# Two blocks of a transformer on one core: first unit by pieces, own operand columns for the last feed-forward trip, no fillers at the first block's seams

## The chip, the cores and the metric

The kernel runs on one core of one Trainium2 chip. The metric is the device time of one execution in microseconds (us); the median of repeated executions is what counts.

## What is computed

256 tokens of width 1024 go through two blocks, all in float32. The reference, cut to its skeleton:

```python
def first_block(x, ...):                    # DEPTH = 2 layers
    for i in range(DEPTH):
        h = h + 0.5 * swiglu(rmsnorm(h), ffn1)           # d_ff 2816
        u = rmsnorm(h)                                   # w_in: conv, low-rank q/kv, two gates
        merged = sigmoid(g_conv) * short_conv(u) + sigmoid(g_mla) * mla_attention(u)
        h = h + merged @ w_o
        h = h + 0.5 * swiglu(rmsnorm(h), ffn2)
        h = h + sigmoid(rmsnorm(h) @ w_ple_gate) * (p @ w_ple_proj)
    return rmsnorm(h)

def second_block(x, ...):                   # a layer with GLA, then one with NSA
    for i in range(DEPTH):
        h = gla_mixer(x) if i == 0 else nsa_mixer(x)
        x = layer_norm(ALPHA * x + h)
        x = layer_norm(ALPHA * x + moe_ffn(x))           # 16 experts in 4 groups, top 2
```

## The kernel before

Everything sits in SBUF as features on 128 partitions by 256 tokens; `h` is the residual stream. The program is five instruction streams written by hand, one per engine, that meet in semaphores; program order on each engine is the order of execution. Weights come as a stream of **units** of 128x2048 floats (1 MB). SP fetches each unit in two halves into one of three `raw` slots. ACT rounds it to `w_hi` (`split_hi`), DVE writes the rest as `w_lo` (`split_lo`), and PE takes the unit (`take`). Activations are split in the same way, into `x_hi`/`x_lo` or `y_hi`/`y_lo`, so one exact product is three matmuls (hi by hi, hi by lo, lo by hi; `product`, L1897). The splits run two units ahead of PE, and the slot of a unit is the one of the unit three before it.

A **dense** unit (`columns`) multiplies two blocks of 128 output columns by 8 pieces of the operand: 48 matmuls of 256 columns. The operand becomes ready in four pieces of two (`PIECES`), one `x_ready` each. With `first_wait=STARTS` PE waits for a piece where the first output block needs it; the second block is done only after the first.

A **feed-forward** stage has 11 trips of 256 hidden columns. A trip of PE is `gate_up(0)` (gate), `gate_up(1)` (up), each 16 pairs of matmuls (L1994 with 512 and L1995 with 256 columns), and `down` of the trip before (48 matmuls). DVE and ACT make the hidden operand in between: DVE `side` (L1239), ACT its rounding (L866), DVE the rest (L1244). That operand has two columns of 256, always the same ones, so ACT waits for the `down` before it. The last `down` stands behind the loop, after six fillers. A **filler** (`keep_warm`, L1946) is a matmul of zeros whose result nobody reads.

`units(n, after)` of DVE is: split of a coming unit, wait for a result, use of the result (`after`). With `early=True` the last of them uses the result first and splits behind it.

The stages that the change touches are called **seams** here, where PE goes from one stage to the next and needs an operand made from the last result: end of ffn1 to `w_in`; the rope of the queries (`query`, L1406 to L1416, which reads PSUM banks that the keys' unit writes next); `w_mla_out` to `w_o` (`merge`, L1429); `w_o` to ffn2 (`residual`, L1438); end of ffn2; the embedding gate to the next layer's ffn1 or, after the second layer, to GLA; and in the second block the start and end of an expert stage (`moe`) and the start of NSA. The layer loop runs the first block's code twice. An expert stage has 20 tiles of three units; POOL copies token slots of a run of four tiles (`copy_runs`, L691) and PE reads three register values (`value_load`) that tell which slots a run uses.

## Time and profile before

| | |
|---|---|
| median of 3 runs (lowest to highest) | 2005.53 us (2005.04 to 2006.02) |
| time of the profiled execution | 2010.71 us |
| its span | 2008.9 us |
| PE, DVE, ACT, POOL busy | 98%, 71%, 55%, 2% of the span |
| granted clock, mean over the span | 0.99 |

PE is the engine to watch: its busy share holds the fillers and whatever runs at half clock, so 98% is not 98% useful. The useful views are who PE waits for, the stretches around each seam instruction by instruction, and the granted clock of short stretches.

### The profile page before, as it was taken

The page shows a single profiled execution, that of the slowest core. Times are in us where ns is not written, and L with a number is a line of the kernel's source. Part 1 is how long each engine was busy: PE and PEld are TensorE (multiplying, and loading weights), DVE is VectorE, ACT ScalarE, POOL GpSimd, SP SyncE. Part 2 cuts the span into 40 slices and gives each one's busy share as a digit, 9 for nine tenths or more (in the row PEclk, how much of TensorE's full clock was granted, in tenths as well). Part 3 has the DMA queues.
Part 4 walks back from the last instruction along what each step waited for, and adds up shares of the span by engine and source line. Part 5 has one row for each costly group of instructions (what it writes and reads, how often), then busy time and mean ns, then how long its engine had stood idle before and what let it go on. Part 6 is the DMA issues. An engine that isn't in the chain of part 4 may idle for free.

```text
span 2008.9 us, 34438 instructions
## 1 busy us (share of the span) xinstructions
PE 1969.5 (98%) x12986; PEld 1775.3 (88%) x12986; DVE 1434.0 (71%) x1812; ACT 1099.2 (55%) x1449; POOL 33.6 (2%) x37
## 2 busy tenths in 40 slices
PE   9999999999999999999999999999999999999999
PEld 7999998989988999999988999888888788997887
DVE  6666876666667766786666667685788877568886
ACT  6444645454447544545545446434677643646775
POOL 0000000000000000000000000000100011001000
PEclk9999999999999999999999999999999999999999
DMA  7655554346554655555345556352799744027993
GB/s 280 200 185 187 178 196 148 130 157 196 184 185 161 192 185 187 191 184 171 115 164 179 188 188 191 123 163 69 277 367 366 288 126 139 9 96 307 367 368 140
DMA packets 89662, 388.03 MB, mean 193 GB/s; under 512 B 10096, under 2 KB 10096, under 8 KB 74832
## 3 DMA queue, kind: packets, MB, share of 16 engines
q1 hardware_dynamic: 88992, 383.87, 55.9%
q0 software_dynamic: 560, 2.67, 0.3%
q8 instruction: 73, 1.20, 0.2%
q14 instruction: 37, 0.30, 0.1%
HBM read 385.45 MB, written 1.05 MB: 192 GB/s over the span
## 4 chain that ended last, share of the span: by engine, by line
PE 89%; DVE 5%; ACT 2%; issue 2%; DMA 1%; DVEq 1%; SPq 0%; ACTq 0%
PE psa L1897 36%; PE psd L1897 19%; PE psa L1994 16%; PE psa L1995 8%; DMA raw<-weights 1%; DVE w_lo L1142 1%; PE psa L2522 1%; PE psa L2195 1%; DVEq L1127 1%; PE psd L1939 1%; PE psd L2531 1%; PE psa L2100 0%; PE psd L2049 0%; DVE x_both L1155 0%; PE psd L2215 0%
## 5 line engine op out<-in xcount | busy, mean ns | idle before, releaser
L1142 DVE TENSOR_TENSOR w_lo<-raw,w_hi 128x1024 fp32r<-128x1024 f32 x500 | 593.4, 1229 | 128.3 <-ACT w_hi L758 125.9
L1897 PE MATMUL psa<-x_both,w_hi 128*128 128x256 f32 x1984 | 366.3, 287 | 9.2 <-DVE x_both L1147 4.2
L758 ACT ACTIVATE w_hi<-raw 128x1024 fp32r<-128x1024 f32 x250 | 262.7, 1051 | 181.4 <-PE psa L1897 179.5
L1897 PEld LDWEIGHTS psa<-x_both,w_hi 128*128 128x128 f32 x1984 | 313.1, 194 | 13.3 <-DVE x_both L1155 5.6
L1897 PE MATMUL psa<-x_both,w_lo 128*128 128x256 f32 x992 | 282.4, 285 | 0.0
L760 ACT ACTIVATE w_hi<-raw 128x1024 fp32r<-128x1024 f32 x250 | 261.3, 1045 | 3.5 <-DMA raw<-weights 3.5
L1994 PE MATMUL psa<-x_both,w_hi 128*128 128x512 f32 x704 | 248.4, 395 | 4.1 <-DVE x_both L1155 1.7
L1994 PE MATMUL psa<-y_both,w_hi 128*128 128x512 f32 x704 | 249.6, 396 | 1.6 <-DVE y_both L1155 1.6
L1897 PE MATMUL psa<-w_hi,slots_x 128*128 128x512 f32 x640 | 204.8, 401 | 0.0
L1995 PE MATMUL psa<-x_both,w_lo 128*128 128x256 f32 x704 | 197.7, 281 | 0.0
L1995 PE MATMUL psa<-y_both,w_lo 128*128 128x256 f32 x704 | 196.8, 280 | 0.0
L1897 PEld LDWEIGHTS psa<-x_both,w_lo 128*128 128x128 f32 x992 | 192.1, 194 | 0.0
L1994 PEld LDWEIGHTS psa<-x_both,w_hi 128*128 128x128 f32 x704 | 132.6, 188 | 34.6 <-issue 3.6
L1994 PEld LDWEIGHTS psa<-y_both,w_hi 128*128 128x128 f32 x704 | 132.1, 188 | 33.2 <-DVE y_both L1155 2.2
L1897 PE MATMUL psd<-y_both,w_hi 128*128 128x256 f32 x816 | 151.2, 286 | 4.7 <-DVE w_lo L1142 4.3
L1137 DVE TENSOR_TENSOR w_lo<-raw,w_hi 128x2048 fp32r<-128x2048 f32 x60 | 137.5, 2292 | 16.2 <-ACT w_hi L753 14.0
L1897 PE MATMUL psd<-x_both,w_hi 128*128 128x256 f32 x768 | 139.1, 283 | 0.4 <-DVE x_both L1244 0.4
L1897 PEld LDWEIGHTS psa<-w_hi,slots_x 128*128 128x128 f32 x640 | 117.2, 188 | 25.0
L1897 PEld LDWEIGHTS psd<-y_both,w_hi 128*128 128x128 f32 x816 | 128.3, 192 | 6.9 <-DVE w_lo L1142 4.7
L1995 PEld LDWEIGHTS psa<-x_both,w_lo 128*128 128x128 f32 x704 | 133.7, 190 | 0.1
L1995 PEld LDWEIGHTS psa<-y_both,w_lo 128*128 128x128 f32 x704 | 132.1, 188 | 0.2
L1897 PE MATMUL psa<-w_lo,slots_x 128*128 128x512 f32 x320 | 126.8, 396 | 0.0
(402 smaller groups left out, 3452.4 us busy)
## 6 DMA issues: line engine op xcount, KB each, us to landing
raw<-weights SPq DMA_DIRECT2D x500, 512.0 KB, 5.0
raw<-weights SPq DMA_DIRECT2D x60, 1024.0 KB, 5.3
raw_y<-weights SPq DMA_DIRECT2D x36, 1024.0 KB, 5.2
x<-weights SPq DMA_DIRECT2D x18, 1024.0 KB, 4.9
h<-x_in SPq DMA_DIRECT2D x1, 1024.0 KB, 5.2
result<-h SPq DMA_DIRECT2D x2, 512.0 KB, 2.9
sml<-smalls POOLq DMA_DIRECT2D x1, 831.0 KB, 10.3
cst<-consts POOLq DMA_DIRECT2D x1, 747.5 KB, 7.7
```

The source lines that it names most:

```text
L758: act.activation(w_hi[:, s, UNIT_HALVES[0]], raw[:, s, UNIT_HALVES[0]], ACT.Copy).then_inc(hi_done, 1)
L760: act.activation(w_hi[:, s, UNIT_HALVES[1]], raw[:, s, UNIT_HALVES[1]], ACT.Copy).then_inc(hi_done, 1)
L1127: dve.drain()
L1137: dve.tensor_tensor(w_lo[:, s, :], raws[r], w_hi[:, s, :], ALU.subtract).then_inc(lo_done, 2)
L1142: dve.tensor_tensor(w_lo[:, s, c], raw[:, s, c], w_hi[:, s, c], ALU.subtract).then_inc(lo_done, 1)
L1897: ins = pe.matmul(out, lhs, rhs, start=first and n == 0, stop=last and n == 2, skip_group_check=True)
L1939: ins = pe.matmul(out, ones, src[:, k, :], start=k == 0, stop=k == n - 1)
L1994: pe.matmul(out, hi, operand[2][:, :, k, :], start=k == 0, stop=False, skip_group_check=True)
L1995: ins = pe.matmul(out[:, 0:T], lo, operand[0][:, k, :], start=False, stop=k == KD - 1, skip_group_check=True)
L2195: ins = pe.matmul(out[:, P * tt:P * tt + keys], a, b, start=False, stop=tt == 1 and n == len(terms) - 1, skip_group_check=True)
L2522: ins = pe.matmul(out[:, P * tt:P * tt + keys], nsa_q[:, i, tt * P:tt * P + P], (nsa_ks, nsa_kw)[branch][:, i // 4, side_of, 0:keys], star ...
L2531: ins = pe.transpose(psd[:, t % 2, P * i:P * i + P], nsa_probs[:, t % 3, P * i:P * i + P], ident)
```

## The change

It joins these edits. (1) `columns` with `STARTS` and the first `gate_up` of a feed-forward stage take the operand piece by piece: all output blocks of a piece before the next piece. (2) The last trip of a feed-forward stage is written out behind the loop (9 trips in the loop and one behind it where there were 10), and its hidden operand goes to columns 2 and 3 of the buffer, so it need not wait for the `down` before it; the split of the next stage's unit comes behind it on ACT and DVE. (3) The 6, 8 and 8 fillers at the seams of the first block go; in an expert stage's start 5 and 9 become 8 and 6. (4) `query` makes its four products first and writes them to `x32`; the combining comes after the next split. (5) `merge` and `residual` lose `early=True`. (6) In the first expert stage's last tile two of the three splits of coming units move behind the tile's hidden operand, one of them behind the layer norm. (7) The NSA gates' 16 products are made during the layer norm, piece by piece, in another PSUM bank, with a semaphore `mix_known` of their own. (8) POOL's copy for run r waits for the r+1st `turn` of the stage, and PE's register reads come one per tile. The diff of these, cut to its core:

```diff
                 for run in range(1, EG):
+                    pool.wait_ge(moe_turned, layer * TILES + run + 1)
...
-                def trip(first):
+                def trip(first, last=False):
...
+                    if last:
+                        act.wait_ge(side_ready, seen.more(side_ready))
+                        act.activation(hid_to[:, 2:4, :], side[:], ACT.Copy).then_inc(hid_hi, 1)
+                        split_hi()
+                        seen.more(unit_done, tag="result")
+                        return
...
-                with seen.loop(act, label, trips - 1):
+                with seen.loop(act, label, trips - 2):
                     trip(False)
+                trip(False, last=True)
...
                     silu(n)
-                    if more or not last:
+                    if more:
                         split_hi()
...
                     hidden_hi(n)
-                    if more:
+                    if more or not last:
                         split_hi()
...
             token_norm(1, scattered, turn_rest, split=True)
-
+            split_hi()
...
-                    if not first:
+                    if not first and not last:
                         split_lo()
                         seen.more(unit_done, tag="result")
+                    to = slice(2, 4) if last else slice(0, 2)
                     dve.wait_ge(hid_hi, seen.more(hid_hi))
-                    dve.tensor_tensor(hid[1][:, 0:2, :], side[:], hid[0][:, 0:2, :],
+                    dve.tensor_tensor(hid[1][:, to, :], side[:], hid[0][:, to, :],
                                       ALU.subtract).then_inc(hid_ready, 1)
+                    if last:
+                        split_lo()
+                        seen.more(unit_done, tag="result")
...
+                turned_q = q_rot.rearrange("p (i e) t -> p i e t", e=2)
+                r1_cos, r2_sin, r2_cos, r1_sin = (x32[:, 2 * i:2 * i + 2, :] for i in range(4))
+
                 def query(j):
-                    c = cos1.unsqueeze(1).broadcast_to([P, 2, T])
-                    s = sin1.unsqueeze(1).broadcast_to([P, 2, T])
                     r1, r2 = four(0, psd)[:, 0:2, :], four(0, psd)[:, 2:4, :]
-                    dve.tensor_tensor(rope_a[:], r1, c, ALU.mult)
-                    step(dve.tensor_tensor(rope_b[:], r2, s, ALU.mult))
-                    turned_q = q_rot.rearrange("p (i e) t -> p i e t", e=2)
-
-                    def combine(to, combined):
-                        for e, part in enumerate((first, second)):
-                            ins = dve.tensor_tensor(turned_q[to, :, e, :], rope_a[part], rope_b[part], combined)
-                        return ins
-                    step(combine(first, ALU.subtract))
-                    dve.tensor_tensor(rope_a[:], r2, c, ALU.mult)
-                    step(dve.tensor_tensor(rope_b[:], r1, s, ALU.mult))
-                    return combine(second, ALU.add)
+                    for dst, r, table in ((r1_cos, r1, cos1), (r2_sin, r2, sin1), (r2_cos, r2, cos1),
+                                          (r1_sin, r1, sin1)):
+                        ins = dve.tensor_tensor(dst, r, table.unsqueeze(1).broadcast_to([P, 2, T]), ALU.mult)
+                    return ins
                 units(1, query)
-                units(3, None)
+                units(1, None)
+                settle()
+                for to, a, b, combined in ((first, r1_cos, r2_sin, ALU.subtract), (second, r2_cos, r1_sin, ALU.add)):
+                    for e, part in enumerate((first, second)):
+                        dve.tensor_tensor(turned_q[to, :, e, :], a[part], b[part], combined)
+                units(2, None)
...
-                units(4, merge, early=True)
+                units(4, merge)
...
-                units(4, residual, early=True)
+                units(4, residual)
...
+            def by_pieces(s, outs, x, ready):
+
+                for piece in PIECES:
+                    pe.wait_ge(ready, seen.more(ready))
+                    for j, out in enumerate(outs):
+                        for k in range(*piece):
+                            c = (k * len(outs) + j) * P
+                            ins = product(out, parts(s, c, c + P), (x[0][:, k, :], x[1][:, k, :]),
+                                          j == 0 and k == 0, k == KD - 1)
+                ins.then_inc(unit_done, 1)
...
+                if first_wait == STARTS:
+                    by_pieces(s, outs, x, ready)
+                    return
...
+                    def block(j, ks):
                         out = psa[:, 2 * bank + j, :]
-                        for k in range(KD):
-                            if j == 0 and k in waits:
-                                pe.wait_ge(x_ready, seen.more(x_ready))
+                        for k in ks:
                             hi, lo = parts(s, (2 * k + j) * P, (2 * k + j + 1) * P)
                             pe.matmul(out, hi, operand[2][:, :, k, :], start=k == 0, stop=False, skip_group_check=True)
                             ins = pe.matmul(out[:, 0:T], lo, operand[0][:, k, :], start=False, stop=k == KD - 1,
                                             skip_group_check=True)
-                        if bank == 1 and j == 0:
+                        return ins
+
+                    s = take()
+                    if waits:
+                        for piece in PIECES:
+                            pe.wait_ge(x_ready, seen.more(x_ready))
+                            for j in range(2):
+                                ins = block(j, range(*piece))
+                    else:
+                        ins = block(0, range(KD))
+                        if bank == 1:
                             ins.then_inc(first_half, 1)
+                        ins = block(1, range(KD))
...
-                            ins = product(out, parts(s, c, c + P), (hid[0][:, k, :], hid[1][:, k, :]),
+                            at = k + 2 if last else k
+                            ins = product(out, parts(s, c, c + P), (hid[0][:, at, :], hid[1][:, at, :]),
...
-                with seen.loop(pe, label, trips - 1):
-
+                def trip():
                     pe.wait_ge(gate_scaled, seen.more(gate_scaled))
                     gate_up(0)
                     pe.wait_ge(side_ready, seen.more(side_ready))
                     gate_up(1)
                     down(False)
+
+                with seen.loop(pe, label, trips - 2):
+                    trip()
+                trip()
                 seen.more(side_ready)
-                pe.wait_ge(gate_scaled, seen.more(gate_scaled))
-                keep_warm(6, psa_of(0))
+                seen.more(gate_scaled)
                 down(True)
...
-                keep_warm(5, psd_of(3))
+                keep_warm(8, psd_of(3))
...
-                keep_warm(9, psd_of(3))
+                keep_warm(6, psd_of(3))
...
-                        pe.wait_ge(group_known, seen.more(group_known))
-                        second = [pe.value_load(second_block[0:1, run:run + 1], min_val=0, max_val=1)
-                                  for run in range(EG - 1)]
                     turn(n - 1)
                     gate_up(n, 1)
+                    if n == 1:
+
+                        pe.wait_ge(group_known, seen.more(group_known))
+                    if n < EG:
+                        second.append(pe.value_load(second_block[0:1, n - 1:n], min_val=0, max_val=1))
                     down(n - 1)
...
-                keep_warm(8, psd_of(0))
                 dense(4, KD, 2, x, signal=None, first_wait=STARTS)
-                keep_warm(8, psd_of(0))
                 feed_forward("ffn2", FF_TRIPS, y, x)
...
-            seen.more(even_normed, 2)
+
+            w_gates = small("w_gates").rearrange("p (k c) -> p k c", k=KD)
+            for j, piece in enumerate(PIECES):
+                ready = (even_normed, odd_normed)[j % 2]
+                pe.wait_ge(ready, seen.more(ready))
+                for k in range(*piece):
+                    for tt in range(TT):
+                        ins = pe.matmul(psd[:, 0, tt * 48:(tt + 1) * 48], h[:, k, tt * P:tt * P + P], w_gates[:, k, :],
+                                        start=k == 0 and tt == 0, stop=k == KD - 1, skip_group_check=True)
+            ins.then_inc(pe_to_act, 1)
...
-            w_gates = small("w_gates").rearrange("p (k c) -> p k c", k=KD)
-            for tt in range(TT):
-                for k in range(KD):
-                    ins = pe.matmul(psa[:, 2, tt * 48:(tt + 1) * 48], h[:, k, tt * P:tt * P + P], w_gates[:, k, :],
-                                    start=k == 0, stop=k == KD - 1, skip_group_check=True)
-            ins.then_inc(pe_to_act, 1)
```

DVE in the rope of the queries, before (`side` and `act_gate` are scratch, `psd` holds the queries' unit, `arena` the tables or the turned queries):

```order
L1142 TENSOR_TENSOR w_lo<-raw,w_hi 128x1024 [waits hi_done]
L1212 REGISTER_ALU
L1406 TENSOR_TENSOR side<-psd,arena 128x512 [waits unit_done]
L1407 TENSOR_TENSOR act_gate<-psd,arena 128x512
L1119 REGISTER_ALU
L1412 TENSOR_TENSOR arena<-side,act_gate 64x2x256 [waits dve_step]
L1412 TENSOR_TENSOR arena<-side,act_gate 64x2x256
L1119 REGISTER_ALU
L1415 TENSOR_TENSOR side<-psd,arena 128x512 [waits dve_step]
L1416 TENSOR_TENSOR act_gate<-psd,arena 128x512
```

The same place now, where `x` is the scratch `x32`:

```order
L1151 TENSOR_TENSOR w_lo<-raw,w_hi 128x1024 [waits hi_done]
L1221 REGISTER_ALU
L1423 TENSOR_TENSOR x<-psd,arena 128x512 [waits unit_done]
L1423 TENSOR_TENSOR x<-psd,arena 128x512 x3
L1150 REGISTER_ALU
L1151 TENSOR_TENSOR w_lo<-raw,w_hi 128x1024 [waits hi_done]
L1150 REGISTER_ALU
L1151 TENSOR_TENSOR w_lo<-raw,w_hi 128x1024 [waits hi_done]
L1430 TENSOR_TENSOR arena<-x 64x2x256 x4
```

The split of the keys' unit moved ahead of the four combining instructions. DVE at the last `merge`, before:

```order
L1429 TENSOR_TENSOR side<-psa,arena 128x512 [waits unit_done]
L1119 REGISTER_ALU
L1430 TENSOR_TENSOR x<-x,side 128x512 [waits dve_step]
L1146 REGISTER_ALU
L1147 TENSOR_TENSOR x_both<-x,x_both 128x512 [waits xh_ready]
L1141 REGISTER_ALU
L1142 TENSOR_TENSOR w_lo<-raw,w_hi 128x1024 [waits hi_done]
L1141 REGISTER_ALU
L1142 TENSOR_TENSOR w_lo<-raw,w_hi 128x1024 [waits hi_done]
```

And now:

```order
L1151 TENSOR_TENSOR w_lo<-raw,w_hi 128x1024 [waits hi_done]
L1221 REGISTER_ALU
L1441 TENSOR_TENSOR side<-psa,arena 128x512 [waits unit_done]
L1128 REGISTER_ALU
L1442 TENSOR_TENSOR x<-x,side 128x512 [waits dve_step]
L1155 REGISTER_ALU
L1156 TENSOR_TENSOR x_both<-x,x_both 128x512 [waits xh_ready]
L1155 REGISTER_ALU
L1156 TENSOR_TENSOR x_both<-x,x_both 128x512 [waits xh_ready]
```

The split that stood between the last two pieces of the operand (`x_both`) stands before the last result now. ACT in the last tile of the first expert stage, before (`act_gate` is the tile's silu, `x_both<-psa` its hidden operand):

```order
L890 ACTIVATE act_gate<-psa 128x256 [waits unit_done]
L758 ACTIVATE w_hi<-raw 128x1024 [waits unit_done,raw_full1]
L760 ACTIVATE w_hi<-raw 128x1024 [waits raw_rest1]
L758 ACTIVATE w_hi<-raw 128x1024 [waits unit_done,raw_full2]
L760 ACTIVATE w_hi<-raw 128x1024 [waits raw_rest2]
L894 ACTIVATE x_both<-psa 128x256 [waits moe_turned]
```

And now:

```order
L899 ACTIVATE act_gate<-psa 128x256 [waits unit_done]
L903 ACTIVATE x_both<-psa 128x256 [waits moe_turned]
L760 ACTIVATE w_hi<-raw 128x1024 [waits unit_done,raw_full1]
L762 ACTIVATE w_hi<-raw 128x1024 [waits raw_rest1]
L912 ACTIVATE slots_x<-psd 128x512 [waits moe_out]
```

The hidden operand comes before both splits now, and the second of them is no longer here.

## Rows read from the trace of the kernel before

**Rows 1.** The page: busy time and share of each engine.

```profile
PE 1969.5 (98%) x12986; PEld 1775.3 (88%) x12986; DVE 1434.0 (71%) x1812; ACT 1099.2 (55%) x1449; POOL 33.6 (2%) x37
```

**Rows 2.** Waits of PE: waiting line, releaser, us in total, times, longest.

```profile
PE psd L1897 <- DVE w_lo L1142: 4.3, 2, 2.1
PE psa L1897 <- DVE x_both L1147: 4.2, 4, 1.8
PE psa L1897 <- DVE x_both L1155: 4.2, 4, 2.2
...
PE psd L1897 <- DVE x_both L1633: 2.9, 1, 2.9
...
PE psa L2144 <- DVE arena L1680: 0.9, 1, 0.9
```

**Rows 3.** Stretches: us, each engine's busy us (instructions), PEclk, DMA share, GB/s.

```profile
321.90:325.30 3.40, 3.40 (x18) 3.40 (x17) 3.40 (x4) 0.00 (x0) 0.00 (x0) 0.50 0.96 261
325.30:328.40 3.10, 3.10 (x27) 3.10 (x26) 0.08 (x1) 0.00 (x0) 0.00 (x0) 1.00 0.92 296
...
1271.41:1277.62 6.21, 6.21 (x29) 6.21 (x30) 5.07 (x6) 5.07 (x5) 0.00 (x0) 0.50 0.02 3
...
1601.90:1605.30 3.40, 3.40 (x10) 2.62 (x10) 0.69 (x1) 0.65 (x2) 0.00 (x0) 0.50 0.95 389
```

**Rows 4.** Chain of waits, the downs of two trips in a row: start, us, what.

```profile
38.63 5.75 PE psd L1897 x48
55.49 5.76 PE psd L1897 x48
```

**Rows 5.** Timeline of PE, end of ffn1: start, us, what, [idle before].

```profile
195.97 1.47 PE L1946 MATMUL psa<-zero 128*128 128x512 bf16 x6
...
210.47 0.81 PE L1939 MATMUL psd<-x,cst 128*128 128x256 f32 x3
```

**Rows 6.** Timeline of DVE at the same end of ffn1.

```profile
192.22 0.69 DVE L1239 TENSOR_TENSOR side<-side,act_gate 128x512 f32<-128x512 f32 x1
...
200.32 1.29 DVE L1260 SCALAR_TENSOR_TENSOR h<-psd,h 128x512 f32<-128x512 f32 x2 [0.19 <-issue]
...
208.90 0.69 DVE L1163 TENSOR_TENSOR x<-x 128x512 f32<-128x512 f32 x1
```

**Rows 7.** Timeline of DVE in the rope of the queries.

```profile
312.99 0.69 DVE L1406 TENSOR_TENSOR side<-psd,arena 128x512 f32<-128x512 f32 x1 [0.18 <-issue]
...
318.48 3.50 DVE L1142 TENSOR_TENSOR w_lo<-raw,w_hi 128x1024 fp32r<-128x1024 f32 x3
```

**Rows 8.** Timeline of PE, then DVE, from w_mla_out to w_o.

```profile
388.37 1.90 PE L1946 MATMUL psd<-zero 128*128 128x512 bf16 x8
...
390.50 2.35 DVE L1142 TENSOR_TENSOR w_lo<-raw,w_hi 128x1024 fp32r<-128x1024 f32 x2
392.77 0.68 DVE L1147 TENSOR_TENSOR x_both<-x,x_both 128x512 fp32r<-128x512 f32 x1
```

**Rows 9.** Timeline of PE, then DVE, from w_o to ffn2.

```profile
414.49 1.90 PE L1946 MATMUL psd<-zero 128*128 128x512 bf16 x8
...
416.09 2.35 DVE L1142 TENSOR_TENSOR w_lo<-raw,w_hi 128x1024 fp32r<-128x1024 f32 x2
```

**Rows 10.** Timeline of DVE, then PE, from the embedding to the next ffn1.

```profile
645.93 0.69 DVE L1163 TENSOR_TENSOR x<-x 128x512 f32<-128x512 f32 x1
...
649.27 0.59 PE L1939 MATMUL psd<-x,cst 128*128 128x256 f32 x2
```

**Rows 11.** Timeline of ACT in the last tile of the first expert stage.

```profile
1596.70 1.06 ACT L758 ACTIVATE w_hi<-raw 128x1024 fp32r<-128x1024 f32 x1 [1.48 <-DMA raw<-weights]
...
1598.97 0.37 ACT L894 ACTIVATE x_both<-psa 128x256 fp32r<-128x256 f32 x1
```

**Rows 12.** One line: the gates' products (ns min/median/max, first and last start, shape).

```profile
L2431 PE MATMUL psa<-sml,h x32: 208/275/275, 1654.3 to 1657.7; 128*128 128x48 f32 x32
```

**Rows 13.** Timeline of DVE beside POOL's first copy of an expert stage.

```profile
1427.51 1.79 DVE L1680 TENSOR_TENSOR arena<-arena 128x32 f32<-128x32 f32 x1
```

33 lines of the change are left out of this document (18 added, 15 removed).

## The prediction

> **What bounds the kernel now.** The page comes first: PE is busy 98% of the span and DVE 71% [rows 1]. So time can leave only through PE: its waits, its fillers, and the stretches where its clock is low. The waits of PE come next [rows 2]. They are few and each sits at a seam: four waits for an operand piece in a dense first unit with 4.2 us in all for each of two lines, two of 2.1 for a weight split, one of 2.9 for the hidden operand of the last expert tile. Then the stretches [rows 3]: after a wide wait the granted clock stands at 0.50 (1.2 GHz) where it is 1.00 (2.4 GHz) otherwise. In 3.40 us at 0.50 PE starts 18 products, in 3.10 us at 1.00 it starts 27, so the low stretch is worth about 3.40 - 18 x 3.10/27 = 1.3 us lost; with the records at its ends left out (16) it is 1.5. I take **1.4 us for one low stretch** and twice that for the 6.2 us one. Last, the timelines around each seam [rows 5 to 13].
>
> Unit prices: 48 products of 256 columns take 5.76 us, 0.12 each, and a trip takes 55.49 - 38.63 = 16.86 us [rows 4], so a gate or up unit is (16.86 - 5.76)/2 = 5.55, or 0.35 for each of its 16 pairs. A piece of one block is 6 x 0.12 = 0.72 in a dense unit and 2 x 0.35 = 0.7 in a gate unit.
>
> **The sum, seam by seam, in us of the profiled execution.** (a) *End of ffn1, twice.* Six fillers and a 0.21 wait stand between the last two `down` [rows 5]: the next product could start at 195.97 and starts 1.68 later. DVE's `side` is done at 192.91 [rows 6]. With columns of its own ACT can round at once (0.63) and DVE subtract (0.7), so the operand is there at about 194.4, before 195.97, and the whole 1.68 goes from this place. What is late next is DVE: the first residual starts at 200.32 because the split of the unit after next lies before it, and that split waits for the slot that the first of the two `down` frees at 196.1. It moves up by the 0.6 by which ACT no longer rounds first, to 199.7. The sum of squares is ready at 208.90 + 0.69 = 209.6 now and 9.3 after that residual; the product over it starts at 210.47. In future it starts at about 209.0, since PE, with both blocks of each piece done as it comes, is through at 208.1. The gain is 210.47 - 209.05 = 1.4; the ends are 0.6 (only DVE's shift) and 2.4 (PE alone). Twice: **2.8**.
>
> (b) *Rope, twice.* DVE holds the queries from 312.99 to 318.48, and PE's keys' unit waits 2.1 for the split behind them [rows 7, 2]. Four products of 0.69 now end at 315.7, and the split (2.36 for two halves) at 318.1, before PE gets there at 318.76. The combining (2.8) comes next, then the split for the values' unit, done at 323.4, which PE needs a keys' unit (5.76) after 318.76, at 324.5. So it has 1.1 left. With the wait of 2.1 goes the low stretch behind it [rows 3]: 2.13 + 1.4 = 3.5. Twice: **7.0**. The lower end, with the clock still low, is 2 x 2.1.
>
> (c) *w_mla_out to w_o, twice.* Eight fillers start at 388.37; the eight hold PE 1.55 before the unit begins at 389.92. Then it waits until 393.5 for the last piece, which DVE makes at 392.77 because the late split (390.50, 2.35) is ahead of it [rows 8]. The split goes into the idle time before the result (it is ready at 384.8), so the last piece is ready at 391.4. PE starts at 388.4 and spends 1.44 on each piece: 389.8, 391.3, then the third piece (ready 390.6), the fourth at 392.7, end 394.2. Now it ends at 389.92 + 5.76 + 1.4 of waits = 397.1. Gain 2.9, twice, with the start 0.1 earlier: **6.0**. (d) *w_o to ffn2, twice.* The same pattern: fillers from 414.49 cost 1.55, and the split at 416.09 stands before the last piece [rows 9]; a wait of 0.8 and the 0.5 of restarts follow. PE now goes through 16 pairs from 414.5 and ends at 420.1 where it ended at 422.9: 2.8, **5.6**. The cover of both is the same: the split must end before the unit's result, with 1.2 to spare in (c).
>
> (e) *End of ffn2, twice.* 1.68 goes as in (a), but the first weight split that the embedding gate needs comes behind DVE's operand and moves only by the same 0.6: **1.2**. (f) *Embedding to ffn1, once.* Half of each of the first two pieces, 2 x 0.7, moves into waits, and a low stretch (1.4) would go. The sum of squares is ready at 646.62 and PE takes it at 649.27 [rows 10]; the gain cannot pass 2.6, and four clears (0.65) come first: **2.3**, or 1.3 with a low stretch. (g) *Embedding to GLA, once.* 2 x 0.72 into waits, and one of the two low stretches of 1271.41 to 1277.62 [rows 3]: **2.8**, ends 2.0 and 3.2.
>
> (h) *Start of the expert stages.* POOL's copy blocks a small product of DVE, 1.79 in place of the 0.19 of its neighbours [rows 13]. In the second stage PE waits 0.9 for that line [rows 2]; in the first it costs 0.5 of a split. Both go; fillers moved from the second place to the first cost about 0.25 each: **0.9**. A register read on PE is hidden behind the products queued before it. (i) *End of the first expert stage.* The hidden operand is rounded at 1598.97, after splits that wait for DMA [rows 11]. The tile's `turn` is done at 1595.9, so the operand is ready at 1596.8 and PE, busy with the first scatter until 1597.8, does not wait: 2.9 [rows 2] and the low stretch behind it [rows 3], 1.4 to 1.5: **4.4**. (j) *Start of NSA.* The gates' 32 passes took 3.6 [rows 12]. They now lie ahead of NSA's first unit; of them 0.9 fits into the longest wait of 1.8 [rows 2], the other 2.7 delay it, and 3.6 goes later, where PE waits 1.6 for a split already. So what comes back is bounded by DVE: between -2 and +2. I take **0**.
>
> **A rule that speaks against part (8).** The row first: beside POOL's copy a DVE product with both inputs in SBUF lasted 1.79 [rows 13]. The copies now run within the tile loop, where nearly every DVE instruction is such a split. The Trainium skill (SBUF — State Buffer, section SBUF: two separate sides) says that VectorE and GpSimd share one port pair under an exclusive lock, that a VectorE operation with two SBUF inputs takes part in it against a GpSimd operation that reads SBUF, and that the later one is fully blocked. By that rule, with which the row agrees, six copies of 1.9 would block up to 11 us of DVE. Not all of it would reach PE: my estimate, from DVE's idle share, is at most 0.9 a copy, 5.4 in all, and a time of 1978. The sum goes by 0, since before the change the second and third copies lay on DVE's work too and PE showed no wait for a split there; 5.4 stays in the range.
>
> **Sum.** 2.8 + 7.0 + 6.0 + 5.6 + 1.2 + 2.3 + 2.8 + 0.9 + 4.4 + 0 = 33.0. The profiled execution took 2010.71, 5.2 above the median of 2005.53 as profiled ones do here; less 33.0 it is 1977.7, and the median **1972.5 us** (faster by 1.6%).
>
> **Rivals.** *1. The clock takes part of it back.* Each filler-free seam may have its own low stretch. For: a wait of 2.1 was enough for one [rows 2, 3], and 0.9 to 1.4 us of waiting is left in (a), (f) and (g), with small products of low activity in (j). Against: in (b), (c) and (d) nothing is left to wait for. Six to nine stretches at 1.4 give 1981 to 1985. *2. The splits do not get there in time.* If the late split in (c) and (d) and the one in (b) still end after PE arrives, by a DMA or a slot, only the fillers and half of the waits go: 3.3 + 3.1 + 3.1 + 4.2 for the first block, about 20 with the rest, 1985 to 1988. For: margins of 1.1 and 1.2. Against: these margins are read from finish times in one timeline. *3. Better:* NSA gives its 2 and (a), (g) reach their upper ends: 1966. *4. Slower than before:* the fillers are what holds the clock in the first block. Its ten seams without fillers would each fall to 1.2 GHz and stay through two stretches and more, as after 1270.8. At 1.4 for a stretch the gain of 33 is gone at 24 stretches; with 28 the time is 2011. Against it: PE has real work in their place. *5. It does nothing:* the waits come from what I did not see, such as fetching instructions for the longer layer body.
>
> **How the numbers follow.** Forecast 0.74 (band 1968 to 1979); rival 1 0.12; rival 2 0.05; rival 3 0.05; rival 4 0.02; rival 5 0.02. The range 1965 to 1984 takes in the forecast's band with the 5.4 of the copies, rival 3 and most of rival 1. About 0.2% (4 us) is what a measurement of this kernel can tell from no change: faster 0.96, same 0.02, slower 0.02.
>
> **What would show it.** In the profile after: no wait of PE at the keys' unit and no low stretch behind it; w_o and ffn2 starting at the spacing of products after the unit before; the two last `down` as 96 products in a row; the last expert `down` directly behind the first scatter; a wait of about 1 us for the folded squares after ffn1; POOL's copies beside longer DVE splits without a wait of PE. It is wrong if the fillers' places show gaps, if low stretches number more than eight, or if NSA's first unit starts over 3 us later against the layer norm.

## Result: 1976.4 us, and the profile after

| | before | changed kernel |
|---|---|---|
| median (lowest to highest) | 2005.28 us (2003.93 to 2006.02), 4 runs | 1976.36 us (1974.0 to 1978.56), 4 runs |
| ratio | 1 | 0.9855, 95% interval 0.9841 to 0.9868 |
| profiled execution | 2010.71 us | 1976.19 us |
| stretches of PE at 1.2 GHz in it | 37.5 us | 13.7 us |

The forecast was 1972.5 with a range of 1965 to 1984. The kernel is faster, by 28.9 us of median where 33.0 were forecast, and the two profiled executions lie 34.5 apart. That these two differences disagree by 5.6 us is the first thing to explain, and the experiments begin there.

The page of the changed kernel, PE's row and the others, to hold beside [rows 1]:

```profile
PE 1944.7 (98%) x12919; PEld 1760.6 (89%) x12930; DVE 1433.3 (73%) x1812; ACT 1099.1 (56%) x1449; POOL 36.7 (2%) x37
```

DVE and ACT do what they did; PE's busy time is 24.8 us shorter. So most of the gain (24.8 of 34.5) is not waiting that went but busy time that went: fillers, and work at 1.2 GHz. The waits of PE by releaser, to hold beside [rows 2]:

```profile
PE psa L1910 <- DVE w_lo L1151: 5.8, 4, 2.0
PE psa L1910 <- DVE x_both L1164: 3.0, 4, 1.5
PE psd L1966 <- DVE x L1172: 1.6, 3, 0.7
...
PE psa L2018 <- DVE w_lo L1151: 1.5, 1, 1.5
```

The line of 4.3 for the split behind the queries and the one of 2.9 for the last expert operand are gone. New are the waits for the folded squares (1.6), which the prediction had named as what is late next after ffn1, two of 1.1 for a split after ffn2, inside the 5.8, and one of 1.5 for a split where the second layer starts. Next come two stretches of the changed kernel at the times of the first and the last of [rows 3] (other instructions run there by now), and the three in which its clock is low (us, each engine's busy us, PEclk, DMA share, GB/s):

```profile
321.90:325.30 3.40, 3.40 (x21) 2.94 (x20) 1.91 (x2) 2.21 (x2) 0.00 (x0) 1.00 0.83 258
...
1383.70:1387.12 3.42, 3.42 (x17) 3.31 (x17) 3.18 (x11) 1.99 (x4) 0.00 (x0) 0.50 1.02 429
1585.10:1591.92 6.82, 6.74 (x31) 6.74 (x32) 5.32 (x5) 4.45 (x6) 4.18 (x6) 0.50 0.38 123
1601.90:1605.30 3.40, 3.40 (x31) 3.40 (x30) 3.23 (x5) 3.17 (x5) 0.00 (x0) 1.00 0.56 188
1772.82:1776.24 3.42, 3.20 (x13) 2.26 (x13) 2.96 (x14) 2.97 (x5) 0.00 (x0) 0.50 1.00 417
```

The first block, which lost its fillers, has no low stretch in this execution. The three that are left (13.7 us) lie around the layer norms and routers of the second block.

The end of ffn1, to hold beside [rows 5, 6], DVE first and then PE:

```profile
197.03 2.36 DVE L1151 TENSOR_TENSOR w_lo<-raw,w_hi 128x1024 fp32r<-128x1024 f32 x2 [0.34 <-ACT w_hi L760]
199.58 1.29 DVE L1274 SCALAR_TENSOR_TENSOR h<-psd,h 128x512 f32<-128x512 f32 x2 [0.19 <-issue]
...
208.16 0.69 DVE L1172 TENSOR_TENSOR x<-x 128x512 f32<-128x512 f32 x1
```

```profile
208.90 1.13 PE L1966 MATMUL psd<-x,cst 128*128 128x256 f32 x4 [0.70 <-DVE x L1172]
```

The residual starts at 199.58, behind the split (199.7 was forecast); PE takes the squares at 208.90 (209.05 was forecast) after a wait of 0.70. The rope, beside [rows 7]:

```profile
311.52 2.48 DVE L1423 TENSOR_TENSOR x<-psd,arena 128x512 f32<-128x512 f32 x4 [0.18 <-issue]
313.93 2.35 DVE L1151 TENSOR_TENSOR w_lo<-raw,w_hi 128x1024 fp32r<-128x1024 f32 x2
316.37 2.79 DVE L1430 TENSOR_TENSOR arena<-x 64x512 f32<-64x512 f32 x4
```

Four products, the split, the combining. The split ends at 316.3, and PE begins the keys' unit at 317.1 without waiting. At w_o, beside [rows 8], the last two operand pieces lie side by side and the split is elsewhere:

```profile
384.58 1.47 DVE L1156 TENSOR_TENSOR x_both<-x,x_both 128x512 fp32r<-128x512 f32 x2
386.31 2.36 DVE L1151 TENSOR_TENSOR w_lo<-raw,w_hi 128x1024 fp32r<-128x1024 f32 x2 [0.26 <-ACT w_hi L760]
```

**The account by seam.** The same instruction of PE was looked up in the trace of before and of the changed kernel at the end of each seam, and the difference of its start times was taken from one seam to the next. The first pair is the two profiled executions above, the second is one more execution of each (the first two experiments).

| step of the sum | forecast | first pair | second pair |
|---|---|---|---|
| (a) end of ffn1, twice | 2.8 | 2.7 | 2.7 |
| (b) rope, twice | 7.0 | 7.6 | 6.1 |
| (c), (d) w_o and ffn2, twice | 11.6 | 11.7 | 11.7 |
| (e) end of ffn2, twice | 1.2 | 1.1 | 1.1 |
| (f) embedding to ffn1 | 2.3 | 1.6 | 0.5 |
| (g) embedding to GLA | 2.8 | 3.2 | 2.0 |
| (h) starts of the expert stages | 0.9 | 1.7 | 0.3 |
| (i) end of the first expert stage | 4.4 | 4.6 | 4.1 |
| (j) start of NSA | 0 | 0.2 | 0.2 |
| the first microseconds, GLA | - | 0.1 | -1.2 |
| sum | 33.0 | 34.5 | 27.4 |

With another instruction taken as the end of a seam these figures move by up to 0.2. Where only instructions and fillers moved (a, c, d, e), both pairs agree with each other and with the sum within 0.2 us. Where a low stretch went (b, f, g, i, which the sum had with one or two each, and h, where it had none), the pairs differ by up to 1.5.

### The profile page after: what moved, and what is told of

The parts are those of the page before. It is cut to its first block, busy times and chain, and to the rows that moved or that the text cites. A ratio compares the mean times of both kernels' runs of the same rounds, so it can differ in the third digit from the quotient of the medians.

```text
span 1974.4 us, 34273 instructions
## 1 busy us (share of the span) xinstructions
PE 1944.7 (98%) x12919; PEld 1760.6 (89%) x12930; DVE 1433.3 (73%) x1812; ACT 1099.1 (56%) x1449; POOL 36.7 (2%) x37
## 4 chain that ended last, share of the span: by engine, by line
PE 90%; DVE 5%; ACT 2%; issue 1%; DVEq 1%; DMA 0%; ACTq 0%; SPq 0%
PE psa L1910 37%; PE psd L1910 19%; PE psa L2018 16%; PE psa L2019 8%; DVE w_lo L1151 1%; PE psa L2564 1%; PE psa L2236 1%; DVEq L1136 1%; PE psd L1966 1%; ACT w_hi L760 1%; PE psd L2573 1%; PE psa L2138 0%; PE psd L2119 0%; PE psd L2256 0%; PE psd L2087 0%
```

## Experiments

Each kernel was timed beside the kernel before. Times are medians with the lowest and the highest run, ratios are against before. The changed kernel had 1974.0 to 1978.6 in eight runs.

**Before, profiled again.** No edit.

> The kernel before, unchanged, profiled a second time. Question: the first profiled execution took 2010.71, 5.2 above the median of 2005.5, and the sum was made against it. Theory A (that execution had more stretches at 1.2 GHz than most): it had nine stretches with 37.5 us in all, mean granted clock 0.990; at 1.4 us lost for 3.4, an execution of 2005.5 has some 12.6 us less of it, 25 us, mean clock 0.994, and the profiled one here lies wherever its number of stretches puts it. Theory B (the profile itself costs some 5 us on this kernel): profiled again about 2010 with the unprofiled runs at 2005. Median 2005 +- 1.5 by both.

Measured: 2005.78 (2003.92 to 2007.06, 11 runs), with 15 more of before between 2002.34 and 2007.35. The profiled execution took 2005.07, with a mean granted clock of 0.993 against 0.990 and eight stretches, 27.3 us where the first had nine with 37.5. So theory A holds: the first profiled execution, 2010.71, was above all 26 others, and the second profiled one, 2005.07, lies in the middle of them, so a profile as such doesn't cost 5 us. The rope's wait in both layers and the stretch behind each show how that comes about (us, busy us of PE, its loads, DVE, ACT and POOL, PEclk, DMA share, GB/s):

```profile
318.20:320.33 2.13, 0.00 (x1) 0.00 (x1) 2.13 (x3) 2.10 (x3) 0.00 (x0) 1.00 0.05 12
320.33:323.73 3.40, 3.40 (x28) 3.40 (x29) 3.40 (x4) 0.82 (x1) 0.00 (x0) 1.00 0.90 290
944.12:946.26 2.14, 0.00 (x1) 0.00 (x1) 2.14 (x3) 2.10 (x3) 0.00 (x0) 1.00 0.06 8
947.40:950.80 3.40, 3.40 (x18) 3.40 (x17) 3.35 (x3) 0.00 (x0) 0.00 (x0) 0.50 0.77 245
```

The wait is the same, 2.13 and 2.14. Behind the first PE runs on at 2.4 GHz and starts 28 products, behind the second it runs at 1.2 GHz and starts 18. In the first profile [rows 3] it was low behind the first as well. So a wait of 2.1 lowers the clock in some executions and not in others, and a low stretch behind it is a price with a chance, not a fixed one.

**The changed kernel again.** No edit.

> The changed kernel, unchanged, as the yardstick for the others here. Median 1976 +- 2, ratio 0.9855. Its first profiled execution (1976.2) had three stretches of 1.2 GHz with 13.7 us in all, none in the first block. Theory A says that the number moves between executions: 3 to 6 stretches of 3.4. A rival (the clock's falls sit at fixed places of the program): the same three places, near 1384, 1585 and 1773.

Measured: 1976.17 (1974.73 to 1977.67), ratio 0.9851 (0.9836 to 0.9866). Four stretches, 17.1 us: the same three places 1.6 us later and one more, behind a wait of GLA that both kernels have. Of the changed kernel's first profile and of this one:

```profile
1287.07:1289.04 1.97, 0.00 (x0) 0.00 (x0) 1.92 (x2) 1.97 (x3) 0.00 (x0) 1.00 0.07 10
1289.04:1292.44 3.40, 3.40 (x15) 2.79 (x16) 3.13 (x3) 2.29 (x3) 0.00 (x0) 1.00 0.80 265
```

```profile
1287.53:1289.50 1.97, 0.00 (x1) 0.00 (x0) 1.92 (x2) 1.97 (x3) 0.00 (x0) 1.00 0.07 10
1289.71:1293.12 3.41, 3.41 (x9) 2.63 (x9) 3.25 (x3) 2.09 (x3) 0.00 (x0) 0.50 0.84 269
```

The same program, the same wait of 1.97, and PE starts 15 products behind it at full clock once, 9 at half clock the other time. Both expectations hold in part: the stretches near 1384, 1586 and 1773 are in both profiles, this one is not.

**The rope alone**, in the kernel before.

```diff
+                    for dst, r, table in ((r1_cos, r1, cos1), (r2_sin, r2, sin1), (r2_cos, r2, cos1),
+                                          (r1_sin, r1, sin1)):
+                        ins = dve.tensor_tensor(dst, r, table.unsqueeze(1).broadcast_to([P, 2, T]), ALU.mult)
...
                 units(1, query)
-                units(3, None)
+                units(1, None)
+                settle()
+                for to, a, b, combined in ((first, r1_cos, r2_sin, ALU.subtract), (second, r2_cos, r1_sin, ALU.add)):
+                    for e, part in enumerate((first, second)):
+                        dve.tensor_tensor(turned_q[to, :, e, :], a[part], b[part], combined)
+                units(2, None)
```

> The kernel before with edit (4) alone: four products of the query first, the combining after the next split. Theory: the wait of 2.1 at the keys' unit goes in both layers (4.2) and the stretch of 1.2 GHz behind it (2 x 1.4), 7.0 in all: 1998.5. Rival: the clock's fall is not caused by that wait and turns up elsewhere: 4.2 only, 2001.3, with as many low stretches as before. Rival 2: the split comes late all the same: 2005.

Measured: 2000.79 (1994.89 to 2001.42, 5 runs), ratio 0.9966 (0.9952 to 0.9979): 4.8 us by the medians, 6.8 by the ratio with an interval from 4.2 to 9.6. That takes in both the 7.0 of the theory and the 4.2 of the first rival, so the time doesn't decide between them. The place itself does: in the second layer, where before's second profile has the low stretch, the instruction behind the rope starts 3.9 earlier against that profile, in the first, where it has none, 2.4. The stretches behind the keys' unit's start:

```profile
318.20:322.00 3.80, 3.80 (x34) 3.80 (x33) 3.76 (x5) 2.92 (x3) 0.00 (x0) 1.00 0.69 235
947.00:951.00 4.00, 4.00 (x30) 3.73 (x30) 3.51 (x4) 1.21 (x1) 0.00 (x0) 1.00 0.60 186
```

PE is busy all the time and at full clock. The waits (4.2) went, and with them what low stretches stood behind them. But the whole profile has as many stretches as before's second, eight, with 34.1 us where that has 27.3, one of them 6.8 us long behind a wait of 1.65 at 637, where before's second profile has none. So the rival's last clause came true in this execution. Its five runs spread over 6.5 us, with mean clocks of 0.991 to 0.997 in them: what is left of the kernel before has its own low stretches, some in one execution and some in another.

**Fillers put back** in the changed kernel, 6, 8 and 8.

```diff
-                seen.more(gate_scaled)
+                pe.wait_ge(gate_scaled, seen.more(gate_scaled))
+                keep_warm(6, psa_of(0))
                 down(True)
...
+                keep_warm(8, psd_of(0))
                 dense(4, KD, 2, x, signal=None, first_wait=STARTS)
+                keep_warm(8, psd_of(0))
                 feed_forward("ffn2", FF_TRIPS, y, x)
```

> The changed kernel with the 6, 8 and 8 fillers of the first block put back at their places. Theory: eight fillers cost 1.55 each time (four times, 6.2), since nothing waits there any more; of the 1.68 before the last `down` 1.2 lies in the waits of 0.5 and 0.7 that the changed kernel has behind it after ffn1, and 1.1 in the one after ffn2, so 0.5 and 0.6 each, 2.2 in all. Sum 8.4: 1984.8. Rival (the fillers hold the clock up, which takes part of the gain back without them): the first block of the changed kernel has low stretches in other executions that the fillers remove; then less than 8.4, down to 0 at six stretches. Rival 2: the waits behind are set by DVE's chain that moves with PE, so the fillers cost their whole 1.68: 12.9, 1989.

Measured: 1983.24 (1982.73 to 1983.34), ratio 0.9888 (0.9873 to 0.9903): 7.1 slower than without. The eights are all of it: against the second profile of the changed kernel PE becomes 3.4 later at w_o and ffn2 of the first layer and 3.4 in the second, 6.9 in all, 1.72 for each eight where 1.55 was reckoned (the 1.55 until the next product starts, and that product takes 0.31 in place of 0.12 to the next). The sixes, for which 2.2 was expected, cost nothing that shows, after ffn1 or after ffn2. After ffn1:

```profile
195.62 1.47 PE L1973 MATMUL psa<-zero 128*128 128x512 bf16 x6
...
208.78 1.13 PE L1966 MATMUL psd<-x,cst 128*128 128x256 f32 x4 [0.19 <-DVE x L1172]
```

13.16 from their start to the squares; in the changed kernel it is 13.16 from the start of the last `down` (189.98 + 5.76) to 208.90. DVE's chain has the place, and the fillers lie in PE's slack (0.19 of the wait of 0.70 is left). The first block had no low stretch with them, as it has none in either profile of the changed kernel without them. In two other kernels without fillers it had one, at 628 and 629, behind PE's wait of 2.0 where the second layer starts, a place at which no filler was taken out.

**The late split back** (edit 5 undone).

```diff
-                units(4, merge)
+                units(4, merge, early=True)
...
-                units(4, residual)
+                units(4, residual, early=True)
```

> The changed kernel with the late split of merge and residual restored (edit 5 undone), still without fillers. Theory: the last operand piece is ready 2.35 later, at 388.4 where PE wants it at 387.2 (w_o) and at 411.2 where PE wants it at 410.3 (ffn2), and behind the latter the folded squares come at 414.0 for a product that starts at 412.4 now. So 1.2 + 1.7 for each layer, 5.8 in all: 1982.0; up to 1.4 more for each wait that lowers the clock. Rival (taking out the fillers was what mattered, the split had room anyway): within 1 of the changed kernel, 1976 to 1977.

Measured: 1978.98 (1977.93 to 1980.25), ratio 0.9869 (0.9853 to 0.9886): 2.8 slower, half of what was expected. PE's two waits in the first layer:

```profile
388.74 0.51 PE L1910 MATMUL psa<-x_both,w_hi 128*128 128x256 f32 x2 [0.68 <-DVE x_both L1156]
...
412.36 0.51 PE L2018 MATMUL psa<-y_both,w_hi 128*128 128x512 f32 x1 [0.40 <-DVE y_both L1164]
```

The last piece at w_o was ready as expected (388.7, expected 388.4), but PE came for it at 388.06 and not at 387.2: the expectation had taken PE's time from the first profile, and in this execution the last result at this seam came 0.5 later. So the waits are 0.68 and 0.40 where 1.2 and 0.9 were worked out. PE takes the squares 1.6 later in each layer, the waits and the shift of the squares together, where 2.9 were expected.

**By output block again** (edit 1 undone): `by_pieces` left out, and the first `gate_up` with its waits in the first output block alone.

```diff
-                if first_wait == STARTS:
-                    by_pieces(s, outs, x, ready)
-                    return
...
                             pe.wait_ge(x_ready, seen.more(x_ready))
-                            for j in range(2):
-                                ins = block(j, range(*piece))
+                            block(0, range(*piece))
+                        ins = block(1, range(KD))
```

> The changed kernel with edit (1) undone: the first unit of a stage finishes its first output block before it begins the second. Theory: at w_o the last piece (ready 386.1) is wanted at 385.1 and not at 387.2, a wait of 1.0; at ffn2 one of 0.6; twice each, 3.2. From the embedding to ffn1 and to GLA half of each of two pieces, 1.4 each, 2.8. After ffn1 nothing, since the squares set the time there. Sum 6.0: 1982.2. Rival (the pieces matter only at the embedding seams): 2.8, 1979. Rival 2 (the clock falls at the longer waits): 6 + 1.4 for each of two to four stretches, 1985 to 1988.

Measured: 1983.34 (1981.51 to 1984.8), ratio 0.9894 (0.9877 to 0.9911): 7.2 slower, with the fillers (7.1) the largest part. Against the first profile of the changed kernel PE loses 0.7 after ffn1 in each layer (1.4), where the expectation had nothing because the squares were to set the time; 1.0 at w_o and 0.8 at ffn2 in each layer (3.6); 0.6 from the embedding to ffn1 (1.4 at the squares, of which 0.8 comes back behind them); and 3.0 to GLA. That is 8.6; from there on this execution has half as much time at 1.2 GHz as the other (6.8 us against 13.7), and in all it is 6.0 longer. What is lost to GLA is more than the pieces alone, for the waits bring a low stretch again:

```profile
1249.59 0.51 PE L1910 MATMUL psa<-x_both,w_hi 128*128 128x256 f32 x2 [2.19 <-DVE x_both L1164]
...
1251.71 0.80 PE L1910 MATMUL psa<-x_both,w_hi 128*128 128x256 f32 x2 [1.14 <-DVE x_both L1164]
```

```profile
1250.83:1257.66 6.83, 5.95 (x28) 5.95 (x29) 5.69 (x9) 5.88 (x6) 0.00 (x0) 0.50 0.00 1
```

2.19 and 1.14 are before's waits at this seam; the changed kernel has 1.47 and 0.43 there and no low stretch in either profile. Over all fourteen profiles of this study the four with the wait of 2.19 have a low stretch here, and the ten with 1.47 have none.

**The splits before the last expert operand** (edit 6 undone).

```diff
                     silu(n)
-                    if more:
+                    if more or not last:
                         split_hi()
...
                     hidden_hi(n)
-                    if more or not last:
+                    if more:
                         split_hi()
...
             token_norm(1, scattered, turn_rest, split=True)
-            split_hi()
```

(and the same three places on DVE)

> The changed kernel with edit (6) undone: the two splits stand before the hidden operand of the last tile of the first expert stage again. Theory: the wait of PE comes back, 2.9 in the first profile of before and 2.4 in the second, and the stretch of 1.2 GHz behind it, 1.4: 3.8 to 4.3, 1980.2. Rival (the low stretch there belongs to the small products of the layer norm, not to the wait, since the changed kernel has it too, 20 us later): only 2.4 to 2.9, 1978.8.

Measured: 1981.58 (1979.32 to 1982.74), ratio 0.9884 (0.9867 to 0.99): 5.4 slower. PE's wait, ACT's cause of it, and the stretch behind:

```profile
1572.56 1.22 PE L1908 MATMUL psd<-w_hi,x_both 128*128 128x512 f32 x2 [3.47 <-DVE x_both L1644]
```

```profile
1568.60 1.06 ACT L760 ACTIVATE w_hi<-raw 128x1024 fp32r<-128x1024 f32 x1 [2.04 <-DMA raw<-weights]
1569.85 1.06 ACT L762 ACTIVATE w_hi<-raw 128x1024 fp32r<-128x1024 f32 x1 [0.19 <-DMA raw<-weights]
1570.82 0.36 ACT L903 ACTIVATE x_both<-psa 128x256 fp32r<-128x256 f32 x1
```

```profile
1572.35:1575.76 3.41, 3.20 (x8) 2.56 (x9) 0.15 (x1) 0.24 (x1) 0.00 (x0) 0.50 1.02 407
```

The hidden operand stands behind splits that wait for weights. The wait is 3.5 here, 2.9 [rows 2] and 2.4 in the two profiles of before: it ends when weights land (ACT waited 2.04 for them here and 1.48 in [rows 11]), and that differs between executions and kernels. Wait and clock are the two parts, as the theory had them; the wait was larger than it said. In the profile PE falls back by 5.2 at this seam, against the 5.4 of the medians.

**The gates back behind NSA's units** (edit 7 undone).

> The changed kernel with edit (7) undone: the 32 passes of the NSA gates behind NSA's units again, not during the layer norm. In the first profile of the changed kernel this seam lost 1.5 against before up to NSA's q and gave back 1.6 later, where before has a stretch of 1.2 GHz at 1694. Theory (prediction's step j: nothing in sum): 1976 +- 1. Rival (the gates at half clock, 5.6 for what took 3.6, are a true loss and the stretch at 1694 is chance): 1974.6.

Measured: 1974.86 (1972.52 to 1975.87), ratio 0.9852 (0.9836 to 0.9869). The median is 1.3 below the 1976.2 of the changed kernel, where the rival had 1974.6, but the ratios are the same (0.9855 and 0.9851 there), so the times alone don't show a gain. First the 32 passes in the changed kernel:

```profile
1581.52 1.09 PE L2462 MATMUL psd<-sml,h 128*128 128x48 f32 x8
1583.09 4.03 PE L2462 MATMUL psd<-sml,h 128*128 128x48 f32 x24 [0.48 <-ACT h L818]
```

Then those of this kernel, and its stretch at the time at which the changed kernel has 1.2 GHz:

```profile
1617.78 3.67 PE L2471 MATMUL psa<-sml,h 128*128 128x48 f32 x32
```

```profile
1585.09:1591.92 6.83, 6.83 (x58) 6.72 (x57) 6.03 (x7) 6.09 (x7) 4.20 (x6) 1.00 0.42 119
```

During the layer norm they take 5.6 from the first to the last, and the 6.8 us from 1585.1 on are at 1.2 GHz. The expectation called the 5.6 half clock, and that is so for the end alone: 24 of the 32 passes start before 1585.1, at 2.4 GHz and 0.11 apart, with a wait of 0.5 for a piece of the layer norm between the first eight and the rest, and the last eight are at 1.2 GHz, 0.21 apart. NSA's first unit starts at 1586.9. With the gates later that unit starts at 1583.0 after an idle wait of 1.8, the same stretch is at full clock (58 matmuls where the changed kernel has 31), and the gates take 3.7. From here to the place behind the gates this profile gains 3.4 on either profile of the changed kernel.

Over all profiles of this study: of nine with the gates during the layer norm, seven have a low stretch that begins between 1585 and 1593 (six of them 6.8 long), and the two of changed kernels with the gates behind have none there. But the kernel before has the gates behind as well, with the same wait of 1.78, and all its three profiles (one with the rope's edit) have a low stretch of 3.4 there. Of the second profile of before, the wait and the stretch:

```profile
1610.00:1611.79 1.79, 0.02 (x1) 0.05 (x1) 1.53 (x3) 1.76 (x4) 0.00 (x0) 1.00 0.00 0
1612.99:1616.40 3.41, 3.41 (x16) 3.41 (x17) 2.36 (x4) 3.14 (x5) 1.30 (x2) 0.50 0.00 0
```

So the wait is followed by a low stretch in three of five, the passes in seven of nine, mostly a longer one. That the small passes as such bring the clock down more often than the wait is not shown.

**The last operand in shared columns, without and with fillers** (edit 2 undone).

```diff
-                    if last:
-                        act.wait_ge(side_ready, seen.more(side_ready))
-                        act.activation(hid_to[:, 2:4, :], side[:], ACT.Copy).then_inc(hid_hi, 1)
-                        split_hi()
...
-                            at = k + 2 if last else k
+                            at = k
```

> The changed kernel with edit (2) undone and no fillers in its place: the last hidden operand goes to the same two columns again, so ACT rounds it only when the `down` before is done, and PE waits with nothing to do at four places. Theory: a wait of 0.63 + 0.7 and a little, 1.5, at each place, but DVE's chain behind it, which sets the squares after ffn1 and the split after ffn2, moves only by the 0.63 of ACT, and the waits of 0.5, 0.7 and 1.1 that the changed kernel has there take the rest: 0.6 at each of four, 2.4: 1978.6. Rival 1 (the wait itself is what counts): 4 x 1.5 = 6.0, 1982.2. Rival 2 (rival 4 of the prediction in small: a filler-free wait of 1.5 lowers the clock): 2.4 + 4 x 1.4 = 8.0, 1984, and a low stretch at 196, 596, 812 and 1212.

> The same with six fillers before the last `down`, as before had it. Theory: the fillers (1.47 and a wait of 0.21) end 0.2 behind the idle wait of the kernel without them and the clock is high in both: within 1 of it, 1979.2. Rival (the fillers hold the clock in that wait): 1978.6 here while the kernel without fillers has 1984. With the kernel that has own columns and the fillers of all three kinds at 1983.2, this one without the eights also tells what the four sixes cost: 1979.2 would leave 4 for the four times eight, against 6.2 by the prediction.

Measured: 1978.39 (1977.56 to 1979.5), ratio 0.9865 (0.9848 to 0.9881), without fillers, and 1977.93 (1977.61 to 1978.22), ratio 0.9863 (0.9846 to 0.9879), with them: 2.2 and 1.8 slower than the changed kernel, the same within their spread. The wait without fillers and the stretch behind it:

```profile
195.83:197.35 1.52, 0.00 (x1) 0.01 (x1) 0.69 (x1) 1.48 (x3) 0.00 (x0) 1.00 0.89 315
197.35:200.75 3.40, 3.40 (x28) 3.40 (x29) 3.09 (x4) 1.05 (x2) 0.00 (x0) 1.00 0.53 174
```

1.52 of idle PE, and 28 products at full clock behind it; so at all four places. The rivals fall: neither the wait itself (6.0) nor the clock (8.0) sets the time, DVE's chain does (0.6 each by the theory, 0.5 each in both profiles). This is the test of rival 4 in small: it covers waits of 1.52, and no run here has longer ones at these places. Between this kernel with the sixes and the one with own columns and all fillers lie 5.3, about the 6.9 of the eights less the 2 of the shared columns.

**POOL's copies at once** (edit 8 undone).

> The changed kernel with edit (8) undone: POOL copies all runs at once at the start of the expert stage and PE reads its three registers in a row; fillers stay at 8 and 6. Theory (step h): the 0.9 wait of PE for the small DVE product in the second stage and the 0.5 in the first come back, 0.9 to 1.4 in all: 1977.4. Rival (the copies now block splits of DVE inside the tile loop, of 1.9 each, as the port rule has it): undoing it gains, up to 5.4, down to 1971; then the tile loops of the changed kernel would be longer than here by that. Rival 2: nothing, because the first tiles give the gain back: in the second stage before lost 1.06 at the start and had 0.75 less at its end.

Measured: 1975.65 (1974.81 to 1976.66), ratio 0.9852 (0.9836 to 0.9869): no difference that can be told, so edit (8) brings nothing that shows, as rival 2 had it, and neither the theory's 1977.4 nor the first rival's 1971 came. The changed kernel's DVE and, below it, POOL, beside a copy:

```profile
1421.86 2.28 DVE L1146 TENSOR_TENSOR w_lo<-raw,w_hi 128x2048 fp32r<-128x2048 f32 x1
...
1425.01 3.02 DVE L1146 TENSOR_TENSOR w_lo<-raw,w_hi 128x2048 fp32r<-128x2048 f32 x1 [0.55 <-ACT w_hi L755]
```

```profile
1423.44 2.46 POOL L693 CAST slots_x<-slots_x 128x2048 fp32r x1 [6.24 <-PE psa L2138]
```

A copy takes 1.90 alone. Here it begins 0.70 before the split beside it ends (1424.14) and takes 2.46, 0.56 more. The next split, 2.28 elsewhere, begins 0.89 before the copy ends (1425.90) and takes 3.02, 0.74 more. So each is held up for nearly the whole time that is left of the other's instruction (0.15 less in both cases), and not for its whole length. The Trainium skill (SBUF — State Buffer, section SBUF: two separate sides) says that whichever of the two starts first has the shared ports for the whole instruction and that the other is fully blocked. The trace agrees to within that 0.15. What it costs DVE is 0.7 a copy and 4.2 for six, and nothing of it can be told in the time: DVE has some idle time before each of these splits (0.55 here).

**Gates and copies back together.**

> The changed kernel with edits (7) and (8) undone together, the version to which the other runs point. Alone they had medians of 1974.9 and 1975.7 where the changed kernel has 1976.2. Theory: the two seams are apart, so the gains of 1.3 and 0.5 add: 1974.4, with the 5.6 of the gates (at 1.2 GHz) in the layer norm gone and no DVE split of 3.0 in the tile loops. Rival 1 (both differences are the spread of the medians, which came from four runs each): 1976 again. Rival 2 (the gates' place at full clock gives back what its profile showed, 3.3, in every execution): 1972.5.

Measured: 1974.52 (1972.77 to 1975.34, 5 runs), ratio 0.9846 (0.9832 to 0.9859). The median is 1.7 below the changed kernel, near the 1974.4 of the theory, and 0.3 below the kernel with the gates alone back, so the copies add nothing that can be told. In its profile the seam of the gates gains 3.4 again, and a low stretch at 1658, right behind them, takes 1.6 of that back. It is the fastest of all here, by a difference that is at the edge of what these runs can tell (the ratios of the changed kernel are 0.9855 and 0.9851, inside the interval of this one).

## Why the prediction was right, and where it was off

**The sum of instructions and fillers was right.** (a), (c), (d) and (e) were worked out from finish times in one timeline and came out at 2.7, 11.7 and 1.1 where 2.8, 11.6 and 1.2 stood. The split for the keys' unit ends 0.9 before PE takes it (0.7 by the prediction's times), the one for the values' unit 1.3 before (1.1 there). The order of who is late next (DVE's residual, then the squares) is what PE waits for now.

**The term that failed is the last one, the step from the profiled execution to the median.** The prediction took the 5.2 between them as a thing "as profiled ones do here". They don't: 2010.71 was an execution with 10.2 us more at 1.2 GHz than before's second profile (37.5 against 27.3), three times 3.4. 3 x 1.4 = 4.2 of the 5.2 is that. The sum of 33.0 was made against such an execution, and for it the sum was even short (34.5). For an ordinary one the gain is 27.4 (the second pair) to 29.4 (the medians beside it). The rows that would have warned were there: three runs within 1 us and a profile 5 above them.

**The low stretches were mis-sized by their chance.** The sum held five of them at 1.4, 7.0 in all, each as certain. The second pair of profiles gives (b) 0.9, (f) 1.8 and (g) 0.8 less than the sum, and before's rope shows why for (b): one and the same wait has the stretch behind it or has it not.

**Steps (f) and (g) overlooked DVE behind the pieces.** At GLA the waits for the operand shrank by 1.43 as forecast (2.19 and 1.14 to 1.47 and 0.43), but a new wait for the squares took 0.8 of it back:

```profile
1250.49 1.13 PE L1966 MATMUL psa<-x,cst 128*128 128x256 f32 x4 [0.81 <-DVE x L1172]
```

So the work itself gives 0.6 here. With one low stretch of before that is the 2.0 of the second pair; the 3.2 of the first pair looks like the forecast of 2.8 only because 6.8 us at 1.2 GHz went there, twice what the sum had. In (f) the first pair gains 2.6 up to the squares, which the prediction called the most that there is, and 1.0 of it is lost behind them, 0.4 in a wait for DVE (L2037). What is left, 1.6, is 1.4 of a low stretch and 0.2 of the work itself; the second pair, with no stretch there, has 0.5, where the sum had 0.9 besides the stretch.

**Step (h)** took a wait of 0.9 out of one line as the gain of edit (8); undone, it costs nothing. In the first pair PE gains 1.1 at that line, and the tiles behind give back 0.7 of it. That the first pair shows 1.7 for this step is luck of the clock: before has 6.8 us at 1.2 GHz at 1410.7 where the changed kernel has 3.4. The second pair, with 3.4 in both, shows 0.3.

**Step (j)** forecast 0 between -2 and +2, and 0.2 was measured, but not by its mechanism. It had NSA's first unit 2.7 later against the layer norm. From the layer norm's products over the statistics to that unit, in before and below it in the changed kernel:

```profile
1613.67 1.38 PE L1980 MATMUL psd<-cst,x 128*128 128x128 f32 x8 [0.31 <-DVE x L1185]
1617.70 0.47 PE L1897 MATMUL psa<-x_both,w_hi 128*128 128x256 f32 x2 [1.78 <-DVE x_both L1147]
```

```profile
1579.27 1.38 PE L2007 MATMUL psd<-cst,x 128*128 128x128 f32 x8 [0.31 <-DVE x L1194]
1586.91 0.77 PE L1910 MATMUL psa<-x_both,w_hi 128*128 128x256 f32 x2
```

It is 4.03 in before and 7.64 in the changed kernel, 3.6 later. The prediction had named over 3 us later there as a sign that it is wrong, and this sign came. What brought the step back to 0.2 is 2.3 from the gates that no longer stand behind the units, and 1.6 from a low stretch that before has at 1694 and the changed kernel has not. With the gates back behind, two profiles gain 3.4 at this seam and one of them keeps 1.8 of it; the medians are 1.3 to 1.7 lower, which the ratios don't confirm.

**The rivals.** Rival 1, the clock takes part back: not by new stretches. Where fillers were taken out, none of the profiles has one, even behind the four idle waits of 1.52 in the kernel with shared columns. What came out less is what the old stretches were worth. Rival 2 fell by the timelines, rival 3 (1966) by the medians, rival 4 by the same profiles (three to five stretches in each and at most one of them in the first block, where it needed 24), rival 5 by the account by seam.

**Still open:** what decides whether a wait of 1.8 to 2.1 is followed by a low stretch. Two profiles of one program differ in it with the same engines busy before; no run here tells it.

## What to carry to other kernels

Before a sum is made against a profiled execution, set its time beside the unprofiled runs: when it is outside their range, look for what it has more of (here low stretches) and take that out of the base. Price a low stretch behind a wait by how often it comes, and price a wait or a filler by what is late next: six fillers of 1.47 cost nothing where DVE's chain had the place, eight cost 1.7 where it had not. An operand taken piece by piece with all its output blocks was worth more (7.2) than the 6.0 worked out from its waits, in part because it also shortened a wait behind which low stretches came (2.2 to 1.5 at GLA). Follow a seam past the first wait that shrinks, to the next result that PE needs: at GLA a wait of 0.8 for the squares took back more than half of what the pieces had saved. And where a forecast of a step comes true, look whether the step's own mechanism did it: (g) in the first pair and (j) in both came out by low stretches that the sum did not have.
